# A hybrid encoder layer with a 32-expert MoE on one core: which rows make a chunk, and the order and grain of the expert weights' loads

## What is computed

```python
h2 = rmsnorm(x, norm_ffn)
logits = h2 @ router_w + router_b            # top 4 of 32, softmax over them: combine
for e in range(32):
    gate = min(h2 @ w_gate[e] + b_gate[e], 7)
    up = clip(h2 @ w_up[e] + b_up[e], -7, 7)
    act = gate * sigmoid(1.702 * gate) * (up + 1)
    y = y + combine[:, e:e + 1] * (act @ w_down[e] + b_down[e])
out = rmsnorm(x + y, norm_final)
```

## Time and profile before

| | |
|---|---|
| median of 3 runs | 1186.99 us (1185.18 to 1187.43) |
| the profiled execution | 1187.47 us, span 1185.6 us |
| mean granted clock of PE | 0.989 |
| busy: PE, DVE, ACT | 1124.1, 364.6, 259.0 us |
| all DMA | 446.81 MB, mean 377 GB/s |

### The profile page before, as it was taken

The page is one execution under the profiler, slowest core; times in us unless marked ns, Lnnn a source line. Parts: engine busy times, 40 slices in busy tenths (PEclk is TensorE's granted clock), DMA queues, the critical chain, the costliest instruction groups (busy, mean ns, idle before and its releaser), DMA issues.

```text
span 1185.6 us, 15352 instructions
## 1 busy us (share of the span) xinstructions
PE 1124.1 (95%) x6077; PEld 563.2 (48%) x6077; DVE 364.6 (31%) x872; ACT 259.0 (22%) x531; POOL 15.8 (1%) x21
## 2 busy tenths in 40 slices
PE   6999999999999999999999998999898989898997
PEld 6998889873333434343434343434343434342442
DVE  4566674741212132222212121212121212121213
ACT  5566565430101111011101010101010101010102
POOL 1000000000000000000000000000000000000000
PEclk9999999999999999999999999999999999999999
DMA  9965546689999999999999999999999999999994
GB/s 285 308 196 162 169 143 252 242 366 388 405 416 428 428 427 429 427 428 428 427 426 427 427 429 426 430 427 428 426 429 425 431 426 430 426 428 427 428 427 197
DMA packets 61617, 446.81 MB, mean 377 GB/s; under 512 B 4742, under 2 KB 33052, under 8 KB 36596
## 3 DMA queue, kind: packets, MB, share of 16 engines
q1 hardware_dynamic: 59066, 439.92, 90.0%
q0 software_dynamic: 1568, 5.51, 1.5%
q10 hardware_dynamic: 922, 0.47, 0.2%
HBM read 444.78 MB, written 1.11 MB: 376 GB/s over the span
## 4 chain that ended last, share of the span: by engine, by line
PE 60%; DMA 35%; DVE 2%; issue 1%; ACT 1%; POOL 0%; SPq 0%; DVEq 0%; ACTq 0%
DMA slot<-in_w_up 34%; PE psum L1139 23%; PE psum L1164 10%; PE psum L829 5%; PE psum L830 4%; PE psum L831 4%; PE psum L1076 4%; PE psum L1091 3%; PE psum L1099 2%; PE psum L907 1%; PE psum L939 1%; PE psum L919 1%; ACT pieces L593 1%; PE psum L1140 1%; DMA raw<-in_w_in 1%
## 5 line engine op out<-in xcount | busy, mean ns | idle before, releaser
L1139 PE MATMUL psum<-slot,xT 128*64 128x512 f32 x1024 | 458.7, 602 | 43.2 <-DMA slot<-in_w_up 42.5
L1140 PE MATMUL psum<-slot,xT 128*64 128x512 f32 x1024 | 459.4, 603 | 0.0
L1139 PEld LDWEIGHTS psum<-slot,xT 128*64 128x64 f32 x1024 | 138.1, 139 | 332.0 <-issue 316.1
L1164 PE MATMUL psum<-slot,guT 128*64 128x512 f32 x992 | 228.1, 602 | 0.2
L1563 DVE COPY gu<-psum 128x512 f32<-128x512 f32 x32 | 33.4, 1045 | 582.4 <-PE psum L1140 582.4
L1140 PEld LDWEIGHTS psum<-slot,xT 128*64 128x64 f32 x1024 | 138.0, 139 | 0.0
L1164 PEld LDWEIGHTS psum<-slot,guT 128*64 128x64 f32 x992 | 66.8, 137 | 135.7 <-issue 117.5
L778 ACT COPY gu<-psum 128x512 f32<-128x512 f32 x32 | 34.0, 1063 | 424.1 <-PE psum L1140 424.1
L829 PE MATMUL psum<-hT_hi,pieces 128*128 128x256 f32 x288 | 83.0, 288 | 1.0 <-ACT qbT L640 1.0
L1295 DVE TENSOR_TENSOR pieces<-raw,pieces 128x2048 fp32r<-128x2048 f32 x31 | 71.6, 2314 | 32.7 <-ACT pieces L593 32.7
L830 PE MATMUL psum<-hT_lo,pieces 128*128 128x256 f32 x288 | 81.4, 283 | 0.0
(11 more groups left out here) (186 smaller groups left out, 920.2 us busy)
## 6 DMA issues: line engine op xcount, KB each, us to landing
slot<-in_w_gate SPq DMA_DIRECT2D x64, 2048.0 KB, 35.8
slot<-in_w_up SPq DMA_DIRECT2D x64, 2048.0 KB, 39.6
slot<-in_w_down SPq DMA_DIRECT2D x61, 2048.0 KB, 36.8
raw<-in_w_in SPq DMA_DIRECT2D x23, 1024.0 KB, 5.4
slot<-in_w_down SPq DMA_DIRECT2D x6, 1024.0 KB, 8.1
windows<-bias_table POOLq DMA_DIRECT2D x14, 384.0 KB, 3.9
raw<-in_w_branch_a SPq DMA_DIRECT2D x4, 1024.0 KB, 5.1
raw<-in_w_out SPq DMA_DIRECT2D x4, 1024.0 KB, 5.5
```

The source lines that it names most:

```text
L1139: mm(bank(GU + nb)[0:CAP, :], x_k, gate[:, c, cols], start=k == 0, stop=k == KC - 1)
L1140: done = mm(bank(GU + nb)[CAP:P, :], x_k, up[:, c, cols], start=k == 0, stop=k == KC - 1)
L1164: done = mm(o[half * CAP:(half + 1) * CAP, :], values[:, k, :], down[:, c, half * BANK:(half + 1) * BANK], start=k == 0, stop=k == KC - 1)
```

## The change

1. **Chunks of every eighth row.** Partition p holds rows 8p to 8p+7 of a whole matrix; chunk c is row 8p+c in each. A half load is now 16 KB out of 32 KB in each partition. `h2`, the router, the gains and the gate and up biases follow this order. The gate and up matmuls read their 512 columns in it too (`of_chunks`): 128 runs of four values at steps of eight, so that one bank of PSUM holds chunks 0 to 3 and the other 4 to 7. `turn_tokens` waits for both column halves.
2. **The ring** has five places of a whole matrix, each filled by two loads of 2 MB. The order is gate, gate, up, up, down, down; a half's place is free when that half of the matrix five places earlier is used (`released`). All issues of SP are written out, with no loop.
3. **Waits of PE.** `gate_up` waits ahead of its first half for both loads of gate and both of up; `step` waits for both loads of down. In experts 30 and 31 (`TAIL`) the loads go gate, up, gate, up as before, and each half waits for its own two (`tail_in`).
4. **Opening.** The first refills (down of expert 1, gate of expert 2) go in steps of 1, 1, 2, 2, 2 chunks. The second round goes by steps of two matrices: half 0 of both, then half 1 of both, once after the opening and once more five places later.
5. **The down bias** is added at the first expert of the last turn (22), no longer at expert 1.

```diff
-ROWS = 4
-PARTS = KC // ROWS
+PARTS = 2
+HALF = KC // PARTS
 LOADS = 3 * PARTS
-RING = 40 // ROWS
+RING = 5
...
+TAIL = 3 * (E - 2)
+MATRICES = [(e, j) for e in range(E - 2) for j in range(3)] + [
+    (E - 2, 0), (E - 2, 1), (E - 1, 0), (E - 1, 1), (E - 2, 2), (E - 1, 2)]
+OPENING = [0, 1, 2, HALF, HALF + 2, KC]
+SPLITS = [2] * RING + [len(OPENING) - 1] * 2
+TURN_TRANSFERS = 3 * TURN_EXPERTS // RING * PARTS
+assert 3 * TURN_EXPERTS % RING == 0 and HEAD + TURNS * TURN_EXPERTS == E and HEAD % 2 == 0
...
-        return o.rearrange("p (i c) -> p i c", c=ROWS)
-    def by_chunk(o):
-        return o.rearrange("p (c i) -> p i c", c=ROWS)
+        return o.rearrange("p (i c) -> p i c", c=KC)
+    def by_chunk(o, half):
+        return o.rearrange("p (c i) -> p i c", c=KC)[:, half * (P // 2):(half + 1) * (P // 2), :]
+    def every(o):
+        return o.rearrange("p (i c) -> p i c", c=HALF)
+    def of_chunks(o, half):
+        return o.rearrange("p (i c) -> p i c", c=KC)[:, :, half * HALF:(half + 1) * HALF]
...
+        def released(m, part):
+            kind = MATRICES[m][1]
+            of_expert = 2 * part + 2 if kind < 2 else part + 1
+            if m < TAIL:
+                return m // 3 * LOADS + (0 if kind < 2 else 2 * PARTS) + of_expert
+            return TAIL // 3 * LOADS + (0, 0, 2 * PARTS, 2 * PARTS, 4 * PARTS, 5 * PARTS)[m - TAIL] + of_expert
...
-            weights_of = [io[name][0].rearrange("e (h p c) n -> e h p (c n)", c=ROWS, p=P)
-                          for name in ("w_gate", "w_up", "w_down")]
-            def load(n, e, j=None):
-                j = n % LOADS if j is None else j
-                h, w = (j // 2, weights_of[j % 2]) if j < 2 * PARTS else (j - 2 * PARTS, weights_of[2])
-                src = w[e, h] if isinstance(e, int) else w[bass.ds(e, 1), h].rearrange("o p n -> (o p) n")
-                i, _ = place_of(n)
-                sp.dma_start(slot[i][:, :, :].rearrange("p c n -> p (c n)"), src).then_inc(slot_in[i], 16)
...
+            weights_of = [io[name][0].rearrange("e (p c) n -> e p c n", c=KC) for name in ("w_gate", "w_up", "w_down")]
+            def load(m, c0, c1, signal):
+                e, kind = MATRICES[m]
+                sp.dma_start(ring[m % RING][:, c0:c1, :].rearrange("p c n -> p (c n)"),
+                             weights_of[kind][e][:, c0:c1, :].rearrange("p c n -> p (c n)")).then_inc(signal, 16)
+            def load_half(m, part):
+                load(m, part * HALF, (part + 1) * HALF, place_in[m % RING])
+            def load_rest(before, first):
+                def free(m, part):
+                    sp.wait_ge(used, before + released(m - RING, part))
+                steps = 0
+                for c0, c1 in zip(OPENING, OPENING[1:]):
+                    if c1 % HALF and first:
+                        steps += 1
+                        sp.wait_ge(first_used, steps)
+                    else:
+                        free(RING + 1, (c1 - 1) // HALF)
+                    for m in (RING, RING + 1):
+                        load(m, c0, c1, place_in[m % RING])
+                for part in range(PARTS):
+                    free(RING + 2, part)
+                    load_half(RING + 2, part)
+                for part in range(PARTS):
+                    free(RING + 4, part)
+                    load_half(RING + 3, part)
+                    load_half(RING + 4, part)
+                for part in range(PARTS):
+                    free(2 * RING, part)
+                    load_half(2 * RING, part)
+                for part in range(PARTS):
+                    for m in (2 * RING + 1, 2 * RING + 2):
+                        free(m, part)
+                        load_half(m, part)
+                for m in range(2 * RING + 3, TAIL):
+                    for part in range(PARTS):
+                        free(m, part)
+                        load_half(m, part)
+                for k in range(2):
+                    for part in range(PARTS):
+                        for m in (TAIL + 2 * k, TAIL + 2 * k + 1):
+                            free(m, part)
+                            load(m, part * HALF, (part + 1) * HALF, tail_in[2 * k + part])
+                for part in range(PARTS):
+                    free(TAIL + 4, part)
+                    load(TAIL + 4, part * HALF, (part + 1) * HALF, tail_in[4 + part])
+                free(TAIL + 5, 1)
+                load(TAIL + 5, 0, HALF, tail_in[6])
+                for half in range(2):
+                    load(TAIL + 5, HALF + half * HALF // 2, HALF + (half + 1) * HALF // 2, last_in[half])
...
             def turn_tokens(tt):
+                pe.wait_ge(h2_left, tt + 1)
+                pe.wait_ge(h2_right, tt + 1)
                 for c in range(KC):
-                    if c % 4 == 0:
-                        pe.wait_ge((h2_left, h2_right)[c // 4], tt + 1)
                     last = tr(bank(2 * tt + c // 4)[:, (c % 4) * P:(c % 4 + 1) * P], h2[:, tt, chunk(c)], ident)
...
             def return_tokens(tt, nb):
-                mm(bank(Y + 2 * tt + nb).rearrange("p (i c) -> p c i", c=ROWS), ident,
-                   h2[:, tt, nb * BANK:(nb + 1) * BANK].rearrange("p (c i) -> p c i", c=ROWS), start=True, stop=False,
-                   skip_group_check=True)
+                mm(bank(Y + 2 * tt + nb).rearrange("p (i c) -> p c i", c=KC), ident,
+                   h2[:, tt, :].rearrange("p (c i) -> p c i", c=KC)[:, :, nb * (P // 2):(nb + 1) * (P // 2)],
+                   start=True, stop=False, skip_group_check=True)
...
-            def arrived(p, n, later):
-                i, turns = place_of(n)
-                pe.wait_ge(slot_in[i], 16 * (p * arrivals(i) + later + (turns + 1)))
-                return slot[i]
+            def arrived(p, m, later):
+                i = m % RING
+                pe.wait_ge(place_in[i], 16 * (p * in_pass(i) + later + in_place(m)))
+                return ring[i]
...
-            def gate_up(p, it, odd, pair, n0, later, y_before, gathers, first=False):
+            def gate_up(p, it, odd, pair, m0, later, y_before, gathers, first=False):
                 for h in range(PARTS):
                     if not odd:
                         pe.wait_ge((xT_half, xT_done)[2 * h // PARTS], pair + 1)
-                    gate, up = arrived(p, n0 + 2 * h, later), arrived(p, n0 + 2 * h + 1, later)
-                    inner = [(c, nb) for c in range(ROWS) for nb in range(2)]
+                    if m0 >= TAIL:
+                        pe.wait_ge(tail_in[m0 - TAIL + h], 32 * (p + 1))
+                        gate, up = ring[m0 % RING], ring[(m0 + 1) % RING]
+                    elif h == 0:
+                        gate, up = arrived(p, m0, later), arrived(p, m0 + 1, later)
+                    inner = [(c, nb) for c in range(HALF) for nb in range(2)]
                     if h == PARTS - 1:
-                        inner = [(c, nb) for nb in range(2) for c in range(ROWS)]
+                        inner = [(c, nb) for nb in range(2) for c in range(HALF)]
                     for c, nb in inner:
-                        k = h * ROWS + c
+                        k = h * HALF + c
                         x_k = xT[:, k, odd * CAP:(odd + 1) * CAP]
-                        cols = slice(nb * BANK, (nb + 1) * BANK)
-                        mm(bank(GU + nb)[0:CAP, :], x_k, gate[:, c, cols], start=k == 0, stop=k == KC - 1)
-                        done = mm(bank(GU + nb)[CAP:P, :], x_k, up[:, c, cols], start=k == 0, stop=k == KC - 1)
+                        mm(every(bank(GU + nb)[0:CAP, :]), x_k, of_chunks(gate[:, k, :], nb), start=k == 0, stop=k == KC - 1)
+                        done = mm(every(bank(GU + nb)[CAP:P, :]), x_k, of_chunks(up[:, k, :], nb), start=k == 0,
+                                  stop=k == KC - 1)
                         if k == KC - 1 and nb == 0:
                             done.then_inc(gu_half, 1)
-                        if first and k == ROWS // 2 - 1 and nb == 1:
+                        if first and nb == 1 and k + 1 in OPENING and (k + 1) % HALF:
                             done.then_inc(first_used, 1)
                     done.then_inc(used, 2)
                     if gathers and h == PARTS // 2 - 1:
...
-                if bias:
-                    pe.wait_ge(early_in, 32)
+                down = arrived(p, m0 + 2, later)
                 for h in range(PARTS):
                     pe.wait_ge(hidden_done, 2 * it + 2 * h // PARTS + 1)
-                    down_part(bank(DOWN), h, arrived(p, n0 + 2 * PARTS + h, later), hidden, before_chunk)
-            def last_two(p, n0, later):
...
                 for e in range(HEAD):
-                    step(p, e, e * LOADS, 0, first=e == 0, bias=e == HEAD - 1)
+                    step(p, e, 3 * e, 0, first=e == 0)
                 def turn(i, final=False):
                     for k in range(TURN_EXPERTS - 2 * final):
-                        step(p, i * TURN_EXPERTS + (HEAD + k), (HEAD + k) * LOADS, i * (TURN_LOADS // RING))
```

(61 more changed lines are left out.)

137 lines of the change are left out of this document (59 added, 78 removed).

## The result

| | before | after |
|---|---|---|
| median of 11 runs each | 1189.19 us (1185.18 to 1191.38) | 1195.23 us (1191.83 to 1196.31) |
| the profiled execution | 1187.47 us, span 1185.6 | 1196.31 us, span 1194.4 |
| mean granted clock of PE | 0.989 | 0.977 |

The ratio is 1.0059 [1.0048, 1.0071]; the forecast was 1193.8 / 1186.99 = 1.0057. The ratio stands for 7.0 us, the two medians lie 6.0 us apart, the two spans 8.8.

A forecast was written before the change was run, and what follows sets the result against it. PE was taken to bound the first part, the weight stream the second, and PE the end. The terms, 8.4 - 2.1 + 0 + 0.5 = +6.8 us on 1186.99, gave 1193.8 us, range 1187.5 to 1200.5.

The forecast's parts named there:

- What bounds the kernel: Whole kernel: PE bounds a first part, the weight stream (427.5 GB/s) the second, PE again after its last wait.
- Term 1: gate_up waiting for whole gate and up: PE's lag behind the stream is paid once, at its end, +8.4 us.
- What would show it: Signs: waits summing 60 to 75 us, expert 30 7 us later, last load 2 us earlier, matmul mean near 602 ns.
- Term 2: Down bias leaving expert 1: 5.3 us off PE's path there (3.62 bias, 1.65 slower down records), hidden at expert 22.
- Term 3: turn_tokens waiting for both column halves, plus turned gate and up biases: expert 0 starts 1.1 us late.
- Term 4: Opening, with finer refills and the bias gone: the stream runs through at 328.9, not 331.0, -2.1 us.
- Term 5: Gate and up matmuls reading 16-byte runs at steps of 32 bytes: taken as 0, bounds 0 and +10%.
- Term 6: PE's clock falling after longer waits, not hidden on expert 29's step: +0.5 us taken, range 0 to 1.65.
- The sum: Whole kernel: 8.4 - 2.1 + 0 + 0.5 = +6.8 us, giving 1193.8 us; chance 0.60.
- strided reads: Rival: strided operand slows gate_up; about 1201 us at +10%, about 1580 at double; chance 0.10.
- a faster or slower stream: Two rivals on the weight stream's rate: faster, 1181 us at 434 GB/s, chance 0.17; 0.5% slower, 1198, chance 0.08.
- slack in experts 30 and 31: Rival: PE finds slack there that the timeline hides, half covering the stricter wait's cost: 1189.6 us; chance 0.05.

The follow-up runs named there:

- b_whole: Kernel before, gate_up waiting for both gate and both up loads in all experts but the last two: 1196.95 us, ratio 1.0065.
- a_half_29: Changed kernel with half waits and load order gate, up, gate, up given back to expert 29 alone: 1189.13 us, ratio to before 1.0004.
- a_half_26: Changed kernel with half waits and load order gate, up, gate, up from expert 26 on: 1185.36 us, ratio to before 0.9971.
- a_half_all: Changed kernel with half waits in every expert and load order gate, up, gate, up from expert 5 on: 1185.42 us, ratio to before 0.998.
- b_bias_22: Kernel before with only the down bias moved from expert 1 to expert 22: 1185.36 us, ratio 0.9982.
- a_bias_1: Changed kernel with the down bias put back at expert 1: 1198.14 us, ratio to before 1.009.
- b_turn: Kernel before with only turn_tokens waiting for both column halves ahead of its loop: 1186.89 us, ratio 0.9995.

## Why the prediction was right, step by step

**What bounds the kernel** held: loads at 426 to 429 GB/s, no shortage after 324 us, PE behind the stream once it ends.

**Term 1**, +8.4 us, held. Expert 30's start moved by 9.85 us: two loads, 9.80; less 1.76 by which the stream leads at expert 29's wait; plus 2.56 for the half clock; less the 0.58 us of waiting that was there; less 0.17 in the rest of the step. (The 7 us named for this start under "What would show it" was too little, by what the clock took and the lead didn't give.) The wait of 0.79 at 1150 is gone, as forecast. Two loads less 0.58, 0.17 and 0.79 are the term: 8.3. b_whole has it alone, a_half_29 and a_half_26 take it away in two steps. The forecast that PE's waits would come once a step and sum to 60 to 75 us failed, at 42.3 us in 12 waits. It took every step's matmuls at full speed, while the half clock behind a long wait stretched them: the gate matmuls were busy 12.0 us longer than before (470.7 for 458.7), and work that runs on leaves less to wait. The bias at expert 22 took a wait as well: there is none between 863.33 and 980.75 us, where the others stand 30 to 60 us apart. That these two make up all that is missing is not shown. From 500 to 1100 us the granted clock was 0.96 with the strict waits, and 0.99 in a_half_all:

```profile
500.00:1100.00 600.00, 558.26 (x2628) 211.28 (x2626) 126.23 (x321) 70.78 (x161) 0.00 (x0) 0.96 1.01 428
```

```profile
500.00:1100.00 600.00, 555.90 (x2661) 217.21 (x2657) 125.93 (x320) 70.75 (x161) 0.00 (x0) 0.99 1.01 428
```

In these 600 us the stream hides it.

**Term 2**, the bias, held, in place and in effect: both shortages after 308 us go with it, by b_bias_22 and a_bias_1. Of the 5.3 us on PE's path only 3.6 are the bias's own. The 1.65 were a clock dip, which b_whole has in that window too (0.89) and a_bias_1 not (1.00), and a_bias_1 loses the same stream without it.

**Term 3**, +1.1 us, was too large: 0.52, all of it the token wait, nothing for the turned biases. The forecast took 0.8 us at tile 0 from the 0.66 us that four transposes last; but what follows starts 0.42 us behind them, and in b_turn the projection moved by 0.47 (246.77 - 244.77 = 2.00 us for 246.05 - 244.52 = 1.53).

**Term 4**, a lead of 2.1 us, was 1.76 at expert 29's wait and 2.3 at the last load. The windows of the opening gave more, 8.0 - 4.2 = 3.8 us, as expert 0 started at 262.22 and not at the forecast 264.1; most of that (1.5 us) is the dip of the shown execution of before. Where the other 2 us went on the way is not settled: over 760 us of full stream they are one GB/s, the last digit of the windows. How much of the lead the finer opening gives, apart from the bias, the runs don't tell: b_bias_22 has 2.3 us from the bias alone. b_whole and b_bias_22 together would give 1.0065 - 0.0018 = 1.0047, the change measured 1.0059; b_whole has 1.0065, a_bias_1 1.009. If anything, what is left of the change (opening, chunks, order) cost 1 to 3 us, but the intervals overlap, and no run has the opening or the chunks alone.

**Term 5**, nothing for the strided operand, held. The changed kernel's line of gate matmuls has the median of before, 592 ns (min, median, max), before and then after:

```profile
L1139 PE MATMUL psum<-slot,xT x1024: 592/592/1085, 263.0 to 1156.9; 128*64 128x512 f32 x171
```

```profile
L1160 PE MATMUL psum<-ring,xT x1024: 592/592/1115, 262.2 to 1165.7; 128*64 128x512 f32 x171
```

Its mean rose from 602 to 617 ns. The prediction had named a rise of this mean as a sign that it is wrong, and the sign was badly chosen: it would have looked like a strided read at +2.5%. The median rules that out, and the count explains the mean: of the 2048 records of gate and up 107 take over 0.75 us, before 38, all in stretches at the lower clock behind waits; 69 more at some 1.06 us for 0.59 raise the mean by 16 ns. SP issues up loads, each pair a pair of experts apart, at 312.05 and 365.10 us, 53.05 us, to the digit the pace of the earlier trace rows:

```profile
312.05 4.28 SPq L464 DMA_DIRECT2D ring<-in_w_up  x2
...
365.10 4.28 SPq L464 DMA_DIRECT2D ring<-in_w_up  x2
```

**Term 6**, the clock, was the term most mis-sized: 0.5 us taken, 1.65 the upper bound, 2.56 measured. The bound came from a dip that PE's full work had met; the one behind a wait of 4.67 us was longer. The trace of before had nearer rows, which the prediction didn't use. Of its nine waits of 2.2 to 3.2 us for a load, five were followed by the lower clock; the one of 2.70 us that ends at 658.00, and the window behind it:

```profile
658.00 1.08 PE L1139 MATMUL psum<-slot,xT 128*64 128x512 f32 x1 [2.70 <-DMA slot<-in_w_up]
...
658.00:660.00 2.00, 2.00 (x6) 0.82 (x8) 0.00 (x0) 0.00 (x0) 0.00 (x0) 0.50 0.96 410
```

**The sum**, +6.8 us, is what the runs show (0.59% of 1187 us is 7.0). The two profiled executions lie 8.8 us apart, 2.0 more than the sum, about what term 6 is short of; that of the changed kernel is the slowest of its 11 runs, so part of this is scatter. Waits, paths and signs came as forecast, but that the number fits to 0.2 us is partly luck: term 6 was short by 2.1 us, term 3 too large by 0.6, and what the rest of the change costs is open. **The rivals** fell: strided reads (592 ns), a faster or slower stream (426 to 429 GB/s from the 12th slice to the 38th; that a pitch of 32 KB loses nothing had no number behind it in the prediction, and these are that number), and slack in experts 30 and 31. From expert 30's start to the last matmul these take 54.92 us for 55.97, and 0.79 of the 1.05 is the wait that is gone.

## What to carry to other kernels

A stricter wait under a stream that bounds the kernel costs nothing while the stream runs; what it adds to the distance between landing and use is paid once, when the stream ends. So coarse waits may stand for most of the loop, but the last steps want the finest grain (here four steps more than the change had; two or three were not run), and the last of them alone isn't enough, as the steps before it hand their lag on. Fixed work belongs out of the part where the engine bounds the kernel and into the part where it waits.

## What was not expected of the hardware

- One wait of 4.67 us brought PE to the lower clock level for some 5 us of work and cost 2.56 us; the waits of 1.75 us and less in the earlier trace rows cost nothing (0.61 to 0.64 us for the first matmul behind them). In between it went either way: in the kernel before, a wait of 2.70 us was followed by the lower clock at 658.00, one of 3.20 us, ending at 717.23, was not (0.61 us). Keeping PE busy with five idle matmuls held the clock at 1.00.
- The clock also falls with no wait over 0.3 us near it, and not in every execution: 0.84 and 0.73 at 252 to 260 us in before, 1.00 in b_bias_22, whose PE code is the same up to there. A start time compared across two single executions was 1.5 us off for this.
- A moving operand read in runs of 16 bytes at steps of 32 bytes ran at the pace of whole rows. So did return_tokens (L1061), which writes PSUM at steps of eight values and reads runs of 64, but for a maximum of 676 ns.

```profile
L1061 PE MATMUL psum<-h,square_sb x8: 592/592/676, 251.6 to 257.8; 128*128 128x512 f32 x8
```

- Loads of 16 KB from every 32 KB kept the rate of one piece: 428 GB/s from 500 to 1100 us in both kernels.
